# A two-layer hybrid decoder on 8 cores: the second MLP matrix cast once in DRAM, output heads copied by ScalarE, residual rows added by accumulating transfers

## The reference, cut to what matters

```
h = layer_norm(alpha * h + square(relu(h @ w1)) @ w2, g, b)      # w1 2048x8192, w2 8192x2048, eps 1e-5
```

## Time and profile before

| | us |
|---|---|
| three runs: lowest, median, highest | 7135.75, 7584.42, 8094.16 |
| the profiled execution | 7121.04 |
| its span (first to last instruction, slowest core) | 7119.2 |
| spans of all cores | 7059.1 to 7119.2 |
| PE busy in the span | 6466.0 (91%) |
| VectorE, ScalarE, POOL busy | 3650.1, 2119.3, 210.3 |

### The profile page before, as it was taken

The page is one execution under the profiler, slowest core; times in us unless marked ns, Lnnn a source line. Parts: engine busy times, 40 slices in busy tenths (PEclk is TensorE's granted clock), DMA queues, the critical chain, the costliest instruction groups (busy, mean ns, idle before and its releaser), DMA issues.

```text
span 7119.2 us, 90560 instructions; the slowest of 8 cores (7059.1 to 7119.2 us)
## 1 busy us (share of the span) xinstructions
PE 6466.0 (91%) x38388; PEld 3278.1 (46%) x38388; DVE 3650.1 (51%) x6211; ACT 2119.3 (30%) x2887; POOL 210.3 (3%) x402
## 2 busy tenths in 40 slices
PE   5898779999899998988999987899998999999788
PEld 3344555554344443433454455555544444444333
DVE  6354535345743335656634555453467333456567
ACT  6213543442533230010131145344425223200101
POOL 0000000000000000000010000000000000000000
PEclk9999989999999999999999998999999999999999
DMA  8320242783543337588671112428734434476884
GB/s 233 75 42 21 55 85 55 146 195 113 191 94 90 83 88 192 127 198 179 135 158 44 29 29 53 97 62 190 197 114 144 99 83 93 107 178 140 216 169 126
DMA packets 264134, 840.84 MB, mean 118 GB/s; under 512 B 29296, under 2 KB 125808, under 8 KB 203568
## 3 DMA queue, kind: packets, MB, share of 16 engines
q0 software_dynamic: 57312, 337.93, 28.0%
q1 hardware_dynamic: 197200, 480.34, 20.6%
q10 hardware_dynamic: 9216, 16.78, 0.7%
HBM read 949.51 MB, written 219.15 MB: 164 GB/s over the span
## 4 chain that ended last, share of the span: by engine, by line
PE 71%; DMA 16%; DVE 9%; ACT 3%; issue 1%; SPq 1%; POOL 0%; DVEq 0%; ACTq 0%; POOLq 0%
PE ps L512 69%; DMA b_npc<-yraw 2%; DMA hres<-b_npc 2%; DMA b_ha<-hd 2%; DMA hres<-b_x 2%; PE ps L516 1%; DMA out<-b_npc 1%; DVE b_y L534 1%; DMA yraw<-b_ym 1%; DMA fb<-b_fst 1%; DMA b_ym<-hres 1%; ACT b_P L519 1%; DMA fa<-b_fst 1%; DVE b_ym L534 1%; DMA b_wup<-up 1%
## 5 line engine op out<-in xcount | busy, mean ns | idle before, releaser
L512 PE MATMUL ps<-b_w2s,b_ha 128*128 128x512 bf16 x4064 | 904.3, 382 | 81.0 <-DVE b_ym L534 70.4
L519 ACT ACTIVATE b_P<-ps 128x1024 bf16<-128x1024 f32 (+4 forms) x784 | 657.2, 856 | 608.2 <-PE ps L512 602.6
L512 PE MATMUL ps<-b_HB,b_w1s 128*128 128x512 bf16 x3072 | 687.4, 380 | 9.1 <-DVE b_y L534 8.9
L512 PEld LDWEIGHTS ps<-b_w2s,b_ha 128*128 128x128 bf16 x4064 | 398.9, 98 | 571.4 <-DVE b_ym L534 74.1
L527 DVE TENSOR_TENSOR b_mtmp<-b_mtmp,ps 128x1024 f32<-128x1024 f32 x192 | 234.5, 1221 | 641.3 <-PE ps L512 641.1
L512 PE MATMUL ps<-b_w2t,b_hs 128*128 128x512 bf16 x2048 | 474.9, 391 | 94.2 <-DVE b_ym L527 50.6
L527 DVE TENSOR_TENSOR b_ym<-b_ym,ps 128x1024 f32<-128x1024 f32 (+1 forms) x326 | 384.4, 1197 | 233.1 <-PE ps L512 233.1
L512 PE MATMUL ps<-b_T,b_Ss 128*128 128x512 bf16 x2048 | 467.8, 382 | 14.7 <-DVE b_small L620 9.4
L512 PE MATMUL ps<-b_wout,b_hT 128*128 128x512 bf16 x2048 | 465.8, 384 | 13.5 <-ACT b_fst L519 7.5
L512 PEld LDWEIGHTS ps<-b_HB,b_w1s 128*128 128x128 bf16 x3072 | 300.6, 98 | 373.2 <-DVE b_y L534 11.1
L519 ACT ACTIVATE b_mjunk<-b_ym 128x512 bf16<-128x512 f32 x128 | 80.6, 630 | 1052.0 <-DVE b_ym L534 1035.1
(11 more groups left out here) (289 smaller groups left out, 9422.2 us busy)
## 6 DMA issues: line engine op xcount, KB each, us to landing
b_w2s<-w POOLq DMA_DIRECT2D x128, 1024.0 KB, 11.4
b_y<-hres SPq DMA_DIRECT2D x64, 1024.0 KB, 6.6
hres<-b_y SPq DMA_DIRECT2D x64, 1024.0 KB, 5.1
b_w1s<-w POOLq DMA_DIRECT2D x64, 1024.0 KB, 8.7
hd<-b_hst SPq DMA_DIRECT2D x128, 512.0 KB, 6.1
b_ha<-hd SPq DMA_DIRECT2D x64, 1024.0 KB, 10.6
b_fw<-wkv POOLq DMA_DIRECT2D x64, 512.0 KB, 7.6
b_ym<-hres SPq DMA_DIRECT2D x128, 256.0 KB, 17.6
```

The lines of the kernel that those rows point to most:

```text
L512: return S.op("pe", lambda e: e.matmul(out, lhsT, rhs, start=start, stop=stop, skip_group_check=True), reads=reads, writes=writes)
L519: return S.op("act", lambda e: e.activation(out, in_, func, **kw), reads=reads, writes=writes)
```

## The change

It has four parts.

1. `w2` is cast once. A new DRAM tensor `w2b` holds `w2` of both layers as bfloat16. `plan_casts` spreads 32 transfers DRAM to DRAM (2 MB read, 1 MB written each) over the 4900 matmuls that follow the C projection of a layer; each is issued on POOL and waits for the matmul at which it stands. `wload` then is a plain load of `w2b` on SyncE.
2. The head of a sum is no longer added to the residual: ScalarE copies PSUM / alpha into `b_ym`, and all later sums are `b_ym` + PSUM / alpha. The result is the sub-layer's input to the norm divided by alpha; the norm's epsilon is divided by alpha squared, which gives the same output.
3. The residual rows are added by accumulating transfers on POOL (512 KB each, 16 per block half), which read the row from `hres` and add it to `b_ym`. Those of a unit with c = 0 are put in a list at its end and issued two after each product of the next unit. The first later sum into the same place waits for them.
4. The transfers of `norm0` go to POOL instead of SyncE. In the prologue the group (28, 29) of block half 1 is put behind the first loads of the down stage, and the `w2` load that takes its slab behind it.

```diff
+    w2_d = dscr("w2b", [DEPTH, 4, 2, 4, 128, 8, 512], BF16)
...
     def mm(out, lhsT, rhs, start, stop, reads, writes):
-        return S.op("pe", ...)
+        tok = S.op("pe", ...)
+        if casts and S.total >= casts[0][0]:
+            k = Tk()
+            k.w = (tok,)
+            casts.pop(0)[1](k)
+        return tok
+
+    def plan_casts(l, first, last):
+        todo = [(c, p, q) for c in range(4) for p in range(2) for q in (0, 1, 3, 2)]
+        for i, (c, p, q) in enumerate(todo):
+            def f(k, c=c, p=p, q=q):
+                S.dma("pool", w2_d[l, c, p, q], W["w2"][l, c, p, q], reads=[k], writes=[w2_tk[l, c, p, q]])
+            casts.append((S.total + first + (last - first) * i // len(todo), f))
...
         phase(f"inD{l}")
+        plan_casts(l, 0, 4900)
...
         def wload(u, q, at):
-            S.dma("pool", b[:, :, :], W["w2"][l, u[1], u[2], q], writes=[b.tk])
+            S.dma("sp", b[:, :, :], w2_d[l, u[1], u[2], q], reads=[w2_tk[l, u[1], u[2], q]], writes=[b.tk])
...
             An["A22"] = aload(0, 0, 3)
+            An["A12"] = aload(0, 0, 1)
+            group([(28, 1), (29, 1)], [])
             Wn["B21"] = wload(u, 2, 169728)
-            An["A12"] = aload(0, 0, 1)
...
-        def resid(k, t, c):
+        def resid(k, t, p):
             T = k * 8 + t
-            S.dma("sp", yap(t, c), hres[src][T * 128:(T + 1) * 128, c * 512:(c + 1) * 512], reads=[hres_tk[src][T]],
-                  writes=[ytk(t, c)])
-        for c in range(4):
-            for t in range(8):
-                resid(0, t, c)
+            tks = [ytk(t, 2 * p), ytk(t, 2 * p + 1)]
+            S.dma("pool", yap(t, 2 * p, 2), hres[src][T * 128:(T + 1) * 128, p * 1024:(p + 1) * 1024],
+                  reads=[hres_tk[src][T]] + tks, writes=tks, accum_op=ALU.add)
...
-                    S.dma("sp", held[i][:, :], yr_d[...
+                    S.dma("pool", held[i][:, :], yr_d[...
...
-                tok = S.dma("sp", dst[t * 128:(t + 1) * 128, c * 512:(c + 1) * 512], p[:, :], reads=[p.tk], writes=w)
+                tok = S.dma("pool", dst[t * 128:(t + 1) * 128, c * 512:(c + 1) * 512], p[:, :], reads=[p.tk], writes=w)
...
                     if head:
-                        stt(y, y, float(ALPHA), v, ALU.mult, ALU.add, yk + bks, yk)
+                        act(y, v, AF.Copy, bks, yk, scale=1.0 / ALPHA)
                     else:
-                        tt(y, y, v, ALU.add, yk + bks, yk)
+                        stt(y, v, 1.0 / ALPHA, y, ALU.mult, ALU.add, yk + bks, yk)
...
             def pieces():
-                for _ in range(4):
-                    if len(back) > 4:
-                        resid(1, *back.pop(0))
+                for _ in range(2):
+                    if rq:
+                        resid(*rq.pop(0))
                 if n0 is not None:
                     next(n0, None)
...
+            if c == 0:
+                rq.extend((k, t, p) for t in range(8))
```

More of the change, by code:

```diff
@@ L144, in op, with dma @@
         return tok
-    def dma(self, q, out, in_, reads=(), writes=()):
+    def dma(self, q, out, in_, reads=(), writes=(), **kw):
         toks = self._gather(q, reads, writes, True)
@@ L156, in dma @@
         ent[1] += 1
-        self.e[q].dma_start(out=out, in_=in_).then_inc(ent[0], 16)
+        self.e[q].dma_start(out=out, in_=in_, **kw).then_inc(ent[0], 16)
         tok = (ent[0], 16 * ent[1], "dma", self._snapshot(q))
@@ L455, in build_program @@
     hd_tk = [[Tk() for _ in range(32)] for _ in range(2)]
+    w2_d = dscr("w2b", [DEPTH, 4, 2, 4, 128, 8, 512], BF16)
+    w2_tk = {(l, c, p, q): Tk() for l in range(DEPTH) for c in range(4) for p in range(2) for q in range(4)}
     yr_d = dscr("yraw", [1024, D], F32)
@@ L502, in build_program @@
     S.op("dve", lambda e: e.memset(epsc[:, :], 1e-5), writes=[epsc.tk])
+    eps2c = cbuf("eps2c", [128, 1], F32)
+    S.op("dve", lambda e: e.memset(eps2c[:, :], 1e-5 / ALPHA ** 2), writes=[eps2c.tk])
     def sm(n=1):
@@ L511, in mm @@
     def mm(out, lhsT, rhs, start, stop, reads, writes):
-        return S.op("pe", lambda e: e.matmul(out, lhsT, rhs, start=start, stop=stop, skip_group_check=True),
-                    reads=reads, writes=writes)
+        tok = S.op("pe", lambda e: e.matmul(out, lhsT, rhs, start=start, stop=stop, skip_group_check=True),
+                   reads=reads, writes=writes)
+        if casts and S.total >= casts[0][0]:
[3 more added lines that the diff above has]
+        return tok
+    casts = []
+    def plan_casts(l, first, last):
[4 more added lines that the diff above has]
+            casts.append((S.total + first + (last - first) * i // len(todo), f))
     def tp(out, in_, reads, writes):
@@ L1863, in mlp_up @@
         group([(30, 0), (31, 0)], [])
-        group([(28, 1), (29, 1)], [])
         tail(group)
@@ L1981, in stats @@
             tt(q, s12[:, :, 1], q, ALU.subtract, bk_, bk_)
-            act(sd, q, AF.Sqrt, bk_ + [epsc.tk], bk_, bias=epsc[:, 0:1])
+            act(sd, q, AF.Sqrt, bk_ + [eps2c.tk], bk_, bias=eps2c[:, 0:1])
             S.op("dve", lambda e: e.reciprocal(r, sd), reads=bk_, writes=bk_)
@@ L2005, in ld @@
                     held[i] = pcs.next()
-                    S.dma("sp", held[i][:, :], yr_d[t * 128:(t + 1) * 128, c * 512:(c + 1) * 512], reads=[yr_tk[t * 4 + c]],
+                    S.dma("pool", held[i][:, :], yr_d[t * 128:(t + 1) * 128, c * 512:(c + 1) * 512], reads=[yr_tk[t * 4 + c]],
                           writes=[held[i].tk])
@@ L2009, in norm0 @@
                 if t == 0:
-                    S.dma("sp", gq[:, :], GB[0][c * 512:(c + 1) * 512].partition_broadcast(128), writes=[gq.tk])
-                    S.dma("sp", bq[:, :], GB[1][c * 512:(c + 1) * 512].partition_broadcast(128), writes=[bq.tk])
+                    S.dma("pool", gq[:, :], GB[0][c * 512:(c + 1) * 512].partition_broadcast(128), writes=[gq.tk])
+                    S.dma("pool", bq[:, :], GB[1][c * 512:(c + 1) * 512].partition_broadcast(128), writes=[bq.tk])
                     if i == 0:
@@ L2058, in mlp @@
         n0 = None
-        queue, back = [], []
+        queue, rq = [], []
         for ui, u in enumerate(units):
@@ L2091, in evac @@
                             i = (k * 8 + t) * 8 + cq
-                            stt(y, y, float(ALPHA) if head else 1.0, bk(b), ALU.mult, ALU.add, [yk, bank[b], acck[i]],
+                            stt(y, bk(b), 1.0 / ALPHA, y, ALU.mult, ALU.add, [yk, bank[b], acck[i]],
                                 [yk, acck[i]], accum_out=acc[:, i:i + 1])
@@ L2098, in evac @@
                                       writes=[yr_tk[t * 4 + cq]])
-                                back.append((t, cq))
-                        elif head:
-                            stt(y, y, float(ALPHA), bk(b), ALU.mult, ALU.add, [yk, bank[b]], [yk])
                         else:
-                            tt(y, y, bk(b), ALU.add, [yk, bank[b]], [yk])
+                            stt(y, bk(b), 1.0 / ALPHA, y, ALU.mult, ALU.add, [yk, bank[b]], [yk])
                     return
@@ L2242, in mlp @@
             pieces()
-            if ui == 7:
-                while back:
-                    resid(1, *back.pop(0))
+            while rq:
+                resid(*rq.pop(0))
+            if c == 0:
+                rq.extend((k, t, p) for t in range(8))
         if last:
```

## The result

The ratio of the changed kernel's time to that of the kernel before is 0.9846, 95% interval [0.9817, 0.9875]: 1.5% faster, where 6958 over 7121, 0.977, was forecast. That is clear of no change, and short of the 2% from which the prediction would have called it faster. Its executions took 7018.88, 7028.31, 7033.48, 7180.70 and 7629.40 us; the profiled one is that of 7028.31, with a span of 7026.8 us on its slowest core, 92.4 us less than the 7119.2 of before; 163 was forecast. The mean of the eight spans fell by 87.8, from 7091.2 to 7003.4.

The account below looks back on a forecast made before the run. PE was taken to be held in the down stages by late VectorE sums into b_ym (177.4 us of waits). 110 + 32 + 5 + 30 - 14 = 163 us gained from 7121 gave 6958 us, range 6905 to 7000.

Parts of the forecast that it names:

- Step 3: Down stages: casting w2 once saves DMA time, but DMA share stays near 0.7 and this alone gains nothing.
- Step 1: Down stages, units 0 and 8: head to ScalarE with the residual later removes the waits; 110 us gained.
- (a): Down stage, first unit: PE waits 16.76 us for a head sum that stood for its residual row.
- (b): Down stage, unit 8: PE waits 31.79 us because a b_ha load was issued late behind residual loads.
- Step 4: Down stages, later units: norm pieces on POOL cycle in 12.9 us for two; 32 us gained.
- (c): Down stages, later units: norm pieces on SyncE stand behind waiting b_ha loads and hold the sums.
- Step 2: Down stages: accumulating residual transfers take 3.3 us each; block half 0 costs nothing.
- Rival 4: Down stages: accumulates are slow, over 6.9 us each; at 12 us, 7286 us in all; chance 0.08.
- Rival 1: Down stages: norm pieces are no faster on POOL, the 63.4 us of waits stay; 6997 us; chance 0.18.
- Step 7: Attention: the casts delay loads that PE wants at once, such as b_wup; 14 us lost, upper end 72.
- Step 5: Prologue order: b_ha loads go out earlier, so PE's waits on b_mtmp mostly go; 5 us gained.
- Rival 2: Down stages, units 8 to 10: head copies wait on ScalarE behind pieces delayed by accumulates; 7026 us; chance 0.11.

Follow-up runs that it names:

- e9: Kernel before with only the w2 casts (placed in MLP up) and plain w2 loads on SyncE; 6993.58 us.
- e11: Kernel before with only the w2 casts (placed in MLP up) and plain w2 loads on POOL; 6960.16, 6966.24 and 6979.24 us.
- e5: Changed kernel without the casts, w2 loads again casting transfers on POOL; 7170.51 us.
- e8: Changed kernel with the head's copies on VectorE instead of ScalarE; 7012.50 and 7019.97 us.
- e4: Changed kernel with all transfers of norm0 back on SyncE; 7027.99 us.
- e3: Changed kernel without the accumulating transfers, residual left out of the sum; down stages fall by 22.1 and 26.6 us.
- e12: Changed kernel with its plain w2 loads issued on POOL instead of SyncE; down stages 938.3 and 852.0 us, +9.8 and +13.7.
- e1: Changed kernel with 31 of 32 casts per layer cut to 16 columns, same places and waits; 6987 to 6995 us.
- e2: Changed kernel with the casts moved whole from the input projection to the start of MLP up; 6996.78 us.
- e10: Changed kernel with casts in MLP up and norm pieces paused in units 9 and 10 but for one each; 6929.01 and 6938.53 us, 0.972 of before.

## Why the prediction was right or wrong

**Step 3 failed: the cast alone was put at nothing.** The prediction said of it: "PE never waits for `b_w2s` in the rows, so this alone gains nothing." It gains 139.0 us of the down stages with its loads on SyncE (e9), 154.2 with them on POOL (e11), more than the 124.9 of the whole change. The tile was never late itself; the relief came to the transfers beside it. The prediction had counted that relief and then misread its own sum: 166 less 42 of 886 us takes 0.14 from the DMA share, to 0.59, and not to "near 0.7". Measured is 0.60.

**Step 1 was right.** With parts 2 to 4 units 0 and 8 lose next to nothing, without part 1 too (e5), so (a) and (b) named waits that these parts remove; neither ScalarE (e8) nor the pieces' queue (e4) has a share in it. What the prediction didn't see is that unit 8 had a second cure: its 30 us came of the residual loads ahead of `b_ha` together with the slow landing, and part 1 alone takes away all but 1 to 5 us of them with the order kept (e9, e11). Unit 0 had no second one: there part 1 leaves 13 to 15 us. Step 6, the restarts, went with the waits: the granted clock of the stages rose from 0.95 and 0.96 to 0.99 and 0.98.

**Step 4 took late pieces for the fault of their queue.** Reading (c) put them behind other loads on SyncE. With that order kept and less traffic they are in time (e11: 0.8 and 0.3 us lost in units 9 to 13, before 47.7 and 41.9). On POOL their store and load were estimated at 5 us each and took 5.5 and 5.6 in units 7 to 15, which makes the cycle some 14.0 us where two products take 13.8. That units 9 to 13 still gained 28.7 us, where 32 and some 7 of restarts were forecast, is luck: part 1 alone gains 80 to 88 there (e9, e11), and the accumulates take 53 back (60.9 lost with them, 8.1 in e3).

**Step 2 was right for block half 0** (no unit from 0 to 8 of the changed kernel is over 48.4 us) and in the price of a transfer, **and too small for half 1:** 14 us a layer were counted in units 9 and 10, and 22.1 and 26.6 lost (e3), restarts included. Rival 4 is refuted: it wants over 6.9 us an accumulate, where 2.8 was measured, and the sixteen of block half 0 held nobody.

**Rival 1 was right that another queue would not help the pieces.** Their queue is worth 8.3 us in the two stages at most (e4). The prediction held against the Trainium skill (DMA: Bandwidth & Descriptors, "Issuing engines are not separate DMA queues") that the queue stood behind waits. The Trainium skill says there that transfers from all issuing engines run on the same 16 DMA engines, so that another issuer saves little. The runs agree with it in size: e4 moved a stage by 5.2 us at most, and POOL for SyncE brought the `w2` loads 6.4 and 8.8 us in e11 and cost 9.8 and 13.7 in e12. Rival 1's other half, dearer starts on POOL, is in part there: from SyncE the pieces' stores and loads landed in 3.9 and 4.6 us (e4). Why is not shown.

**Step 7 was too small:** 14 against 42.7 us in the table, of which 36 go with the casts in e1 and 37.5 in e2; that is a little over half of rival 3's 72. The mechanism, loads that PE wants at once, was right; the list was not. It held `b_wup`, and `b_fw` among the signs, and left out `b_memT` and what `b_P` waits for. The rest, some 6 us in layer 1, stays open.

**Step 5:** MLP up gained 6.9 for 5. But e11, with the old order, has 800.7 in layer 0 too, and e5, with the new one, 800.5 in layer 1, so that the order did it isn't shown.

**The sum.** For the down stages 172 was forecast and 124.9 came; for attention -14, and -42.7 came. That is 47 + 29 = 76 us, where 75 are missing on the mean core (163 - 87.8). Of the 47 some 16 are the base: 215.1 us over the matmuls' time is the slowest core's, and the mean of six cores is 199.5. Some 23 stand in units 9 to 13, where 60.9 us are lost and 38 were to stay (31 and its restarts), and 7 in the last unit of layer 1, which the change doesn't touch. Rival 2's 7026 stands beside the measured 7028, by two terms that it did not hold; its wait on ScalarE in units 8 to 10 is there, at half its price.

## What to carry to other kernels

Where late transfers stand behind every long wait, look at the DMA share of that stretch and not of the stage, and at how long the same number of bytes takes to land there and in a quiet stretch. A tile that is never waited for can still be the cause, by the traffic of its loads. A stall can need both an order and a crowd; then either cure removes it, and two cures do not add up. And when several edits come together, try each alone and each left out, and count the result by place: here the cast gained alone, the other three cured two stalls and made a third longer, and only with the accumulates and the pieces kept apart did all four gain (e10).

## What the runs showed of the hardware

Eight 1 MB blocks took 6.8 us each of all 16 DMA engines as casting loads from 2 MB of float32, and 2.9 as plain loads (before and e11). With the engines 93% busy over 126 us, 256 KB landed in 29.4 us; with the plain loads, at 85% over 105 us, in 8.4. DRAM-to-DRAM casts of 2 MB to 1 landed in 8.8 us, near the estimate of 9; beside them `b_memT`, 1 MB on SyncE, took 18.5 us to land against 10.4 without. Accumulates of 512 KB took some 2.8 us each of the engines and landed in 10.1 to 20.8 us, and cost PE nothing where no pieces shared their time (e10).
